# A hybrid decoder layer: the recurrent half's norm goes to all partitions through a scratch row instead of a diagonal product

## The chip, the core and the metric

The kernel runs on one core of a Trainium2 chip. The metric is the device time of one execution in microseconds (us), lower is better. A core has five engines with queues of their own: TensorE (PE; matrix products and transposes, results into the PSUM banks), VectorE (DVE), ScalarE (ACT), GpSimd (POOL) and SyncE (SP), which here issues every transfer. They wait for each other by semaphores. A transfer counts 16 onto its semaphore when it has landed. PEld is TensorE's loading of its stationary operand, which overlaps its products.

## The reference, cut to what matters

One layer over 256 tokens of 2048 channels, float32: a mixer of two halves, then a mixture of experts, each with a residual. The two halves are eight heads of 128 channels of a gated delta rule, and eight blocks of 128 channels of a gated linear recurrence. The change concerns the second half's norm, the last statements here:

```python
h = rms_norm(x, norm_mix_w)
proj = h @ w_in
q, k, v, z, b, a, rx, rgate = split(proj)
y_gdn = gated_deltanet_group(q, k, v, z, b, a, ...)        # 8 heads
# recurrent half, 8 blocks of 128 channels:
log_a = -8 * r * softplus(-lam)
_, h = associative_scan(lru_combine, (exp(log_a), mult * (i * xc)))
y = h * gelu(gate)
y = rms_norm(y per block of 128 channels, norm_w)
x = x + concat(y_gdn, y_rg) @ w_out
x = x + hierarchical_moe(rms_norm(x))                       # 32 experts, top 2
```

## The kernel before, in words

Activations lie transposed: channels on the 128 partitions, the 256 tokens along the row. So the recurrence is a scan along the row, and the norm of a block is a sum over partitions, one number per token, that has to be multiplied into every partition.

The program has a stretch per head h = 0 to 7. In one stretch three things are interleaved on TensorE by an order written out by hand: the delta rule of head h-1 (`heads`), whose triangular system is solved in levels 1 to 6, the projection of head i = h (six blocks b of 128 columns, `project`, 96 steps of three products each), and small work. `fill(n)` puts n projection steps between two products of a level, so that TensorE has work while ScalarE and VectorE treat a level's result. In each level TensorE makes a product P, ScalarE copies it out of PSUM (L1148, `pm`), TensorE makes a product U from it, and VectorE subtracts it (L1584 to level 4, L1589 at level 5, L1592 at level 6). After level 6 TensorE needs VectorE's L1592 for its next product (L678, `bank<-ew,hT` in the views), which also waits for s_mix.

What ScalarE and VectorE do beside a level stands in `between(n)`, n = 0 to 8, run after level n's own instruction. Weight pieces go through a ring of three: SyncE loads 1 MB, ScalarE copies it in two halves into a rounded form (L1039), VectorE writes the rest (L1438), TensorE uses both, and SyncE may load into the slot again when VectorE is done.

The recurrent half of head h-1 passes through this so: VectorE's `recur` (n = 6) leaves y in `yb`, ScalarE squares it (`y_square`), TensorE sums the squares over partitions into one number per token, with the tokens now on the partitions (`square_sums`). In the next stretch ScalarE takes roots (`roots`, n = 2) and VectorE inverts them into `fi` (`invert`, n = 2): columns 0 and 1 for the delta rule, columns 2 and 3 for the recurrent half, 128 tokens each. Then:

- ScalarE, `scaled`, n = 3: `on` is the delta rule's output times its factor (L1096); `dg` is the identity times columns 2 and 3 (L1099), a diagonal matrix per 128 tokens.
- TensorE, `norms`, at level 3: transposes `on` (L643), and multiplies an all-ones matrix with `dg` (L646), which puts the token's factor on every partition, in bank 6.
- VectorE, `finish`, n = 4: two products into `mixT`, one from bank 7 (L1543), one from `yb`, the norm's weight and bank 6 (L1546), then `silu_z` (L1502).

The helpers of TensorE have one line each in the profile: L563 for products, L566 for transposes. Stretch 1 (`body(1, True)`) has no head before it to finish; the stretches 2 to 7 have `body(i, False)`; the last head's levels have their own lists `between`, with w_out pieces in place of w_in, where n = 5 holds `recur` and `add_early(1)` (L1708), for which TensorE waits. The last head's own norm follows behind its levels.

Behind this come the output projection, the router, and the 32 experts, whose weights (12 MB each) are loaded by SyncE in six pieces.

Of the kernel before, what the change touches and what calls it, by code (L numbers as in the profile page):

```python
# [34 lines left out]
NH = 8  # L35
# [93 lines left out]
def build(nc, ins, out, slots=SLOTS):  # L129
# [4 lines left out]
    with ExitStack() as ctx:  # L134
# [62 lines left out]
        pm = R1b.take(NT, P)  # L197
        on = R1b.take(NT, P)
        dg = R1b.take(NT, P)
        sqy = R1b.take(T)  # L200
        yb = R1b.take(T)

# [29 lines left out]
        stat = sb("stat", [P, 8])  # L232
        rows = sb("rows", [16, 3, P])
        gb = R1b.take(3, P)
        rows_d = nc.dram_tensor("decay_rows", (16, 3 * P), F32, kind="Internal").ap()

        xn = mixT[:, :, :].rearrange("p (t k) i -> p t (k i)", t=NT)
# [140 lines left out]
        s_f = sem("s_f")  # L378
        s_on = sem("s_on")
        s_dg = sem("s_dg")  # L380
        s_oT = sem("s_oT")
        s_rb = sem("s_rb")
        s_ph = sem("s_ph")
# [177 lines left out]
        def _(pe):  # L561
# [77 lines left out]
            def norms(h):  # L639

                pe.wait_ge(s_on, h + 1)
                for t in range(NT):
                    l = tr(bank[7][:, T + t * P:T + (t + 1) * P], on[:, t, :])  # L643
                l.then_inc(s_oT, 1)
                pe.wait_ge(s_dg, h + 1)
                mm(bank[6][:, 0:T], ones, dg.rearrange("p t i -> p (t i)"), True, True).then_inc(s_rb, 1)  # L646

            def heads(h, fill, last_done, nxt):

# [361 lines left out]
        def _(act):  # L1011
# [80 lines left out]
            def scaled(h):  # L1092

                act.wait_ge(s_f, h + 1)
                for t in range(NT):
                    l = act.activation(on[:, t, :], bank[7][:, t * P:(t + 1) * P], ACT.Copy, scale=fi[:, t:t + 1])  # L1096
                l.then_inc(s_on, 1)
                for t in range(NT):
                    l = act.activation(dg[:, t, :], ident, ACT.Copy, scale=fi[:, 2 + t:3 + t])  # L1099
                l.then_inc(s_dg, 1)  # L1100

            def values(h):

# [69 lines left out]
            def body(i, first):  # L1173
                h = i - 1

                def between(n):
                    if n == 0:
                        high(h * 6 + 8, 2, h * 2 + 3, (0,))
                    elif n == 1:
                        factors(h)  # L1180
                        high(h * 6 + 8, 2, h * 2 + 3, (1,))
                    elif n == 2:
                        evac(i, 0)
                        if not first:
                            roots(h - 1)
                        key_norms(h)
                    elif n == 3:
                        values(h)
                        if not first:
                            scaled(h - 1)  # L1190
                        high(i * 6 + 3, 0, i * 2 + 2)
                    elif n == 4:
                        evac(i, 1)
                        tanh_half(i, 0)
                    elif n == 5:
                        high(i * 6 + 4, 1, i * 2 + 2)
                    elif n == 6:
                        evac(i, 2)
                        decays(i)
                        tanh_half(i, 1)  # L1200
                    elif n == 7:
                        y_square(h)
                        high(i * 6 + 5, 2, i * 2 + 2)
                    elif n == 8:
                        squares(i)
                        evac(i, 3)
                        high(i * 6 + 6, 0, i * 2 + 3)
                        tanh_half(i, 2)

                heads(h, between)  # L1210
                evac(i, 4)
                high(i * 6 + 7, 1, i * 2 + 3)
                out_squares(h)
                evac(i, 5)
                gelu_square(i)
                gates(i)
# [24 lines left out]
            def between(n):  # L1241
                h = NH - 1
                if n == 0:
                    mix_high()
                elif n == 1:
                    factors(h)
                    high_out(2)
                elif n == 2:
                    roots(h - 1)
                    key_norms(h)  # L1250
                elif n == 3:
                    values(h)
                    scaled(h - 1)
                    high_out(3)
                elif n in (4, 5, 6):
                    high_out(n)
                elif n == 7:
                    y_square(h)
                    high_out(7)
                elif n == 8:  # L1260
                    mix_high_late()
# [124 lines left out]
        def _(dve):  # L1386
# [153 lines left out]
            def finish(h, rgn):  # L1540

                dve.wait_ge(s_oT, h + 1)
                V.scalar_tensor_tensor(mixT[:, h, :], bank[7][:, T:], gnw[:, 0:1], sz, ALU.mult, ALU.mult)\  # L1543
                    .then_inc(s_mix, 1)
                dve.wait_ge(s_rb, h + 1)
                V.scalar_tensor_tensor(mixT[:, h + NH, :], yb, rgn, bank[6][:, 0:T], ALU.mult, ALU.mult)\  # L1546
                    .then_inc(s_mix, 1)
                dve.wait_ge(s_mix, h * 2 + 2)

            def system(h):  # L1550
# [84 lines left out]
            def body(i, first):  # L1635
                h = i - 1

                def between(n):
                    if n == 0:
                        gates(h)  # L1640
                    elif n == 1:
                        factors(h)
                        rest(h * 6 + 8, 2)
                    elif n == 2:
                        params(i)
                        if not first:
                            invert(h - 1)
                        query_norms(h)
                        conv(i, 0)
                    elif n == 3:  # L1650
                        rest(i * 6 + 3, 0)
                    elif n == 4:
                        if not first:
                            finish(h - 1, rgp[:, 0:1])
                            silu_z(h)
                        silu(i, 0)
                    elif n == 5:
                        rest(i * 6 + 4, 1)
                        conv(i, 1)
                    elif n == 6:  # L1660
                        recur(h)
                        silu(i, 1)
                    elif n == 7:
                        rest(i * 6 + 5, 2)
                        conv(i, 2)

                heads(h, between)
                rest(i * 6 + 6, 0)
                silu(i, 2)
                conv_rx(i)  # L1670
                link(V.tensor_copy(rgp[:, :], ph[:, Q_RGN:Q_RGN + 1]))
                norm_sums(i, True)
                head_params(i)
                system(i)
                rest(i * 6 + 7, 1)
# [10 lines left out]
            def rest_out(m):  # L1686
                rest(NH * 6 + m, m % RING)
# [23 lines left out]
            def between(n):  # L1711
                h = NH - 1
                if n == 0:
                    gates(h)
                    mix_rest(2, lambda a: a[:, 8:12, :])
                elif n == 1:
                    factors(h)
                    rest_out(2)
                elif n == 2:
                    invert(h - 1)  # L1720
                    query_norms(h)
                    add_early(0)
                elif n == 3:
                    rest_out(3)
                elif n == 4:
                    finish(h - 1, rgp[:, 0:1])
                    silu_z(h)
                    rest_out(4)
                elif n == 5:
                    recur(h)  # L1730
                    add_early(1)
                elif n == 6:
                    rest_out(5)
                elif n == 7:
                    rest_out(6)
                    add_early(2)
# [95 lines left out]
            link(V.tensor_scalar(slot[:, :, 0:NE], slot[:, :, 0:NE], -1.0, None, ALU.add))  # L1832
            iota = cst[:, C_IO:C_IO + CAP].rearrange("p (a s) -> p a s", a=1)

            def pick(q, t, j):
                blocks = pickr[:, t, j // 2].rearrange("p (b s) -> p b s", b=3)
                s = slot[:, t, bass.ds(q * QUAD + j, 1)]
                if j % 2 == 0:
# [3 lines left out]
            def picks(q):  # L1842

                for t in range(NT):
                    for j in range(QUAD):
                        l = pick(q, t, j)
                l.then_inc(s_pick, 1)

            def gates_of(q):
# [3 lines left out]
            if CAP < SLOTS:  # L1853
                link(V.memset(pick, 0.0))
            V.tensor_reduce(cnt[:, 0:1], bank[5][:, 2 * NE:3 * NE], AX.X, ALU.max).then_inc(s_cnt, 1)
            pick(0, 0, 0)
            dve.wait_ge(s_cnt, 1)
            V.tensor_scalar(cnt[:, 1:2], cnt[:, 0:1], float(CAP), 1.0, ALU.is_gt, ALU.add).then_inc(s_cnt, 1)
            pick(0, 0, 1)
            for q in range(2, T // CAP):  # L1860
                dve.wait_ge(s_cnt, q)
                V.scalar_tensor_tensor(cnt[:, 1:2], cnt[:, 0:1], float(q * CAP), cnt[:, 1:2],
                                       ALU.is_gt, ALU.add).then_inc(s_cnt, 1)
                if q < 4:
                    pick(0, 0, q)
            dve.wait_ge(s_cnt, T // CAP)
            V.tensor_copy(nrounds[:, :], cnt[:, 1:2]).then_inc(s_nr, 1)
            for j in range(QUAD):
                l = pick(0, 1, j)
            l.then_inc(s_pick, 1)  # L1870

            dve.wait_ge(s_route, 1)
# [145 lines left out]
```

## Time and profile before

| | |
|---|---|
| Time, 3 runs | median 1473.07 us (1470.9 to 1474.52) |
| Profiled execution | 1471.94 us, its span 1470.1 us |
| Mean granted TensorE clock | 0.985 |
| TensorE busy | 1355.3 us (92%) |
| VectorE busy | 611.1 us (42%) |
| ScalarE busy | 440.0 us (30%) |
| Transfers | 481.63 MB, mean 328 GB/s |

The span runs from the first to the last instruction. The shares are averages over very different stages: up to about 450 us the heads run, then the output projection and the router, and from about 527 us the experts. A busy time counts instructions, not how well an engine is used; which engine's work ends last in a stage stands in the chain of waits.

### The profile page before, as it was taken

How to read it: one execution, taken by the hardware profiler on the slowest of the kernel's cores; microseconds unless marked ns; L12 is line 12 of the kernel's file. 1: busy time of each engine (PE TensorE's matmuls, PEld its weight loads, DVE VectorE, ACT ScalarE, POOL GpSimd, SP SyncE). 2: the span in 40 equal slices, each digit the busy share in tenths (PEclk: the TensorE clock that was granted, in tenths of full speed). 3: DMA queues.
4: the chain of work that ended last, by engine and by line, in shares of the span. 5: the costliest groups of instructions: out<-in, count | busy, mean ns of one | idle time of the engine just before them, and what ended most of it. 6: DMA issues, size and time to landing. Idle time of an engine off the chain costs nothing.

```text
span 1470.1 us, 20406 instructions
## 1 busy us (share of the span) xinstructions
PE 1355.3 (92%) x7784; PEld 834.5 (57%) x7784; DVE 611.1 (42%) x1136; ACT 440.0 (30%) x865; POOL 65.3 (4%) x63
## 2 busy tenths in 40 slices
PE   4999999999999998899999899899899889999895
PEld 3899999999988743343353343343353344335332
DVE  5977787778855621232223212222222122222323
ACT  5465655656554511111021011020111111102102
POOL 0012220122100000000000000000000000000000
PEclk9999999999999999999999999999999999999999
DMA  7565555455546769999999999999999999999994
GB/s 201 152 155 152 151 148 152 120 150 151 200 144 192 313 261 428 429 428 428 426 428 428 428 429 428 429 428 429 428 428 428 429 428 424 429 428 428 427 428 191
DMA packets 147064, 481.63 MB, mean 328 GB/s; under 512 B 11385, under 2 KB 112978, under 8 KB 121810
## 3 DMA queue, kind: packets, MB, share of 16 engines
q1 hardware_dynamic: 147026, 481.10, 83.8%
q8 instruction: 26, 0.43, 0.1%
q14 instruction: 12, 0.10, 0.0%
HBM read 478.96 MB, written 2.12 MB: 327 GB/s over the span
## 4 chain that ended last, share of the span: by engine, by line
PE 66%; DMA 24%; DVE 5%; ACT 2%; issue 1%; SPq 1%; DVEq 0%; ACTq 0%
PE bank L563 65%; DMA ew<-in_expert_w_dram 23%; PE bank L566 2%; DVE w_parts L1438 1%; ACT ew L1350 1%; DMA fw<-in_norm_ffn_w_dram 1%; SPq L530 0%; DVE fw L1907 0%; ACT fw_r L1277 0%; DVE ew L1477 0%; DVE fw_r L1758 0%; DVE fw L1398 0%; DVE fw L1958 0%; DVE ew L1915 0%; ACT ew L1352 0%
## 5 line engine op out<-in xcount | busy, mean ns | idle before, releaser
L563 PE MATMUL bank<-ew,hT 128*64 128x512 f32 (+1 forms) x1568 | 466.6, 602 | 39.5 <-DMA ew<-in_expert_w_dram 32.3
L563 PEld LDWEIGHTS bank<-ew,hT 128*64 128x64 f32 (+1 forms) x1568 | 156.8, 141 | 336.3 <-issue 336.0
L563 PE MATMUL bank<-act_parts,w_parts 128*128 128x256 f32 x2304 | 308.0, 288 | 1.7 <-DVE w_parts L1438 1.7
L563 PEld LDWEIGHTS bank<-act_parts,w_parts 128*128 128x128 f32 x2304 | 285.1, 191 | 2.9 <-issue 1.4
L563 PE MATMUL bank<-ew 128*64 128x512 f32 (+2 forms) x1120 | 248.8, 574 | 6.8 <-DVE ew L1917 6.8
L563 PE MATMUL bank<-mixT,hT 128*64 128x512 f32 x512 | 227.0, 596 | 0.0
L1915 DVE SCALAR_TENSOR_TENSOR ew<-ew,bank 128x256 f32<-128x256 f32 x32 | 13.5, 421 | 453.9 <-ACT ew L1352 453.9
L563 PEld LDWEIGHTS bank<-ew 128*64 128x64 f32 (+1 forms) x1120 | 84.8, 141 | 147.4 <-issue 137.2
L1438 DVE TENSOR_TENSOR w_parts<-fw,w_parts 128x2048 fp32r<-128x2048 f32 x64 | 147.7, 2312 | 31.5 <-ACT w_parts L1039 30.5
L1367 ACT ACTIVATE ye_r<-bank 64x512 fp32r<-64x512 f32 x128 | 68.8, 585 | 279.6 <-PE bank L563 278.8
L1350 ACT ACTIVATE ew<-bank,gs 128x512 f32<-128x512 f32 x32 | 22.0, 687 | 422.0 <-PE bank L563 422.0
L1039 ACT ACTIVATE w_parts<-fw 128x1024 fp32r<-128x1024 f32 x128 | 128.6, 1053 | 12.5 <-PE bank L563 9.0
L1935 DVE TENSOR_TENSOR cst_r<-bank,ye_r 64x512 fp32r<-64x512 f32 x64 | 41.3, 684 | 112.5 <-ACT ye_r L1367 112.3
L1935 DVE TENSOR_TENSOR act_parts<-bank,ye_r 64x512 fp32r<-64x512 f32 x64 | 41.3, 684 | 99.2 <-ACT ye_r L1367 99.0
L1907 DVE TENSOR_TENSOR fw<-fw,bank 128x512 f32<-128x512 f32 x128 | 77.8, 678 | 0.8 <-PE bank L563 0.8
L563 PE MATMUL bank<-act_parts,fw_r 128*128 128x256 f32 x384 | 71.9, 300 | 1.7 <-DVE act_parts L1840 1.3
L563 PE MATMUL bank<-w_parts,act_parts 128*128 128x512 f32 x288 | 69.7, 395 | 0.3 <-DVE fw L1708 0.3
L563 PEld LDWEIGHTS bank<-mixT,hT 128*64 128x64 f32 x512 | 69.9, 138 | 0.0
L1971 POOL TENSOR_TENSOR hT<-ew,cst 128x256 f32<-128x256 f32 x48 | 54.1, 1160 | 283.1 <-DVE ew L1557 283.1
L563 PEld LDWEIGHTS bank<-act_parts,fw_r 128*128 128x128 f32 x384 | 59.9, 201 | 6.6 <-DVE hT L1896 3.8
L563 PE MATMUL bank<-ye_r,act_parts 128*128 128x512 f32 x128 | 58.2, 455 | 5.3 <-DVE act_parts L1935 3.3
L563 PE MATMUL bank<-hT 128*128 128x128 f32 x416 | 62.0, 274 | 0.0
(245 smaller groups left out, 1088.5 us busy)
## 6 DMA issues: line engine op xcount, KB each, us to landing
ew<-in_expert_w_dram SPq DMA_DIRECT2D x160, 2048.0 KB, 16.1
mixT<-in_expert_w_dram SPq DMA_DIRECT2D x32, 2048.0 KB, 18.5
fw<-in_w_in_dram SPq DMA_DIRECT2D x48, 1024.0 KB, 6.0
fw<-in_w_out_dram SPq DMA_DIRECT2D x16, 1024.0 KB, 5.1
mixT<-in_x_dram SPq DMA_DIRECT2D x1, 2048.0 KB, 7.9
fw<-in_x_dram SPq DMA_DIRECT2D x1, 2048.0 KB, 9.6
out_dram<-fw SPq DMA_DIRECT2D x4, 512.0 KB, 2.7
hT<-decay_rows SPq DMA_DIRECT2D x8, 192.0 KB, 5.7
```

The source lines that it names most:

```text
L563: return nc.tensor.matmul(o, l, r, start=start, stop=stop, skip_group_check=True)
L566: return nc.tensor.transpose(o, i, ident[0:n, 0:n])
L1039: act.activation(wparts[:, slot, 0, cols], raw[:, slot, cols], ACT.Copy).then_inc(s_high, 1)
L1350: act.activation(hs, bank[2][:, :], ACT.Copy, scale=gs[:, j:j + 1]).then_inc(s_hs, 1)
L1367: act.activation(y_hi[side * 64:side * 64 + 64, side ^ (j % 2), i * 512:(i + 1) * 512], bank[4 + i][side * 64:side * 64 + 64, :], ACT.Copy ...
L1438: V.tensor_tensor(wparts[:, slot, 1, :], raw[:, slot, :], wparts[:, slot, 0, :], ALU.subtract).then_inc(s_restD, 1)
L1907: V.tensor_tensor(x2c, x2c, bank[COMB[i % 4]][:, :], ALU.add).then_inc(s_add[t], 1)
L1915: V.scalar_tensor_tensor(eth, eth, 1.0, b3[:, :, 0:SLOTS], ALU.add, ALU.mult).then_inc(s_u, 1)
L1935: l = V.tensor_tensor(y_lo[half][rows, cols], bank[4 + i][rows, :], y_hi[rows, half, cols], ALU.subtract)
L1971: G.tensor_tensor(atm[:, lv], A[:, 1, 0:3:2, :], m.broadcast_to([P, NT, P]), ALU.mult).then_inc(s_atm, 1)
```

## The change

The norm's factor of the heads 0 to 6 no longer passes through `dg` and TensorE. ScalarE writes the two columns of `fi` to a scratch row in device memory (two transfers of 128 numbers), and at n = 4, one level further on, waits for both and issues a transfer that reads the row into all 128 partitions, at the place of `dg`. VectorE's `finish` and `silu_z` move from n = 4 to n = 5 and multiply with that copy. The last head keeps the diagonal product. A helper `pick` is renamed `seat`, which changes nothing in the program that runs.

```diff
+        rr = dg.rearrange("p t i -> p (t i)")
+        norm_d = nc.dram_tensor("norm_row", (1, T), F32, kind="Internal").ap()
+        s_ro = sem("s_ro")
+        s_rr = sem("s_rr")
...
@@ TensorE, norms(h)
-                pe.wait_ge(s_dg, h + 1)
-                mm(bank[6][:, 0:T], ones, dg.rearrange("p t i -> p (t i)"), True, True).then_inc(s_rb, 1)
+                if isinstance(h, int) and h == NH - 1:
+                    pe.wait_ge(s_dg, 1)
+                    mm(bank[6][:, 0:T], ones, dg.rearrange("p t i -> p (t i)"), True, True).then_inc(s_rb, 1)
@@ ScalarE, scaled(h)
-                for t in range(NT):
-                    l = act.activation(dg[:, t, :], ident, ACT.Copy, scale=fi[:, 2 + t:3 + t])
-                l.then_inc(s_dg, 1)
+                if isinstance(h, int) and h == NH - 1:
+                    for t in range(NT):
+                        l = act.activation(dg[:, t, :], ident, ACT.Copy, scale=fi[:, 2 + t:3 + t])
+                    l.then_inc(s_dg, 1)
+                else:
+                    for t in range(NT):
+                        act.dma_start(norm_d[:, t * P:(t + 1) * P].rearrange("a p -> p a"), fi[:, 2 + t:3 + t])\
+                            .then_inc(s_ro, 16)
+
+            def norm_row(h):
+
+                act.wait_ge(s_ro, h * 32 + 32)
+                act.dma_start(rr, norm_d.broadcast_to([P, T])).then_inc(s_rr, 16)
@@ ScalarE, between(n) of the bodies
                     elif n == 4:
+                        if not first:
+                            norm_row(h - 1)
                         evac(i, 1)
                         tanh_half(i, 0)
@@ ScalarE, between(n) of the last head
                 elif n in (4, 5, 6):
+                    if n == 4:
+                        norm_row(h - 1)
                     high_out(n)
@@ VectorE, finish(h, rgn)
-                dve.wait_ge(s_rb, h + 1)
-                V.scalar_tensor_tensor(mixT[:, h + NH, :], yb, rgn, bank[6][:, 0:T], ALU.mult, ALU.mult)\
-                    .then_inc(s_mix, 1)
+                if isinstance(h, int) and h == NH - 1:
+                    dve.wait_ge(s_rb, 1)
+                    r = bank[6][:, 0:T]
+                else:
+                    dve.wait_ge(s_rr, h * 16 + 16)
+                    r = rr
+                V.scalar_tensor_tensor(mixT[:, h + NH, :], yb, rgn, r, ALU.mult, ALU.mult).then_inc(s_mix, 1)
@@ VectorE, between(n) of the bodies
                     elif n == 4:
-                        if not first:
-                            finish(h - 1, rgp[:, 0:1])
-                            silu_z(h)
                         silu(i, 0)
                     elif n == 5:
                         rest(i * 6 + 4, 1)
                         conv(i, 1)
+                        if not first:
+                            finish(h - 1, rgp[:, 0:1])
+                            silu_z(h)
@@ VectorE, between(n) of the last head
                 elif n == 4:
+                    rest_out(4)
+                elif n == 5:
                     finish(h - 1, rgp[:, 0:1])
                     silu_z(h)
-                    rest_out(4)
-                elif n == 5:
                     recur(h)
                     add_early(1)
```

## Rows read from the trace of the kernel before

**Rows 1.** Chain of waits, heads: start us, us, engine and what, line

```profile
176.84 4.11 PE bank L563 x35
...
181.17 41.41 PE bank L563 x339
...
424.38 0.69 DVE fw L1708
425.06 0.14 issue
425.20 23.79 PE bank L563 x113
```

**Rows 2.** Stretches: busy us per engine (instructions), granted clock, DMA share, GB/s

```profile
176.00:222.00 46.00, 46.00 (x381) 45.31 (x380) 35.85 (x64) 27.77 (x60) 7.62 (x7) 1.00 0.57 144
...
600.00:1427.00 827.00, 763.80 (x3656) 329.81 (x3652) 198.01 (x400) 124.23 (x254) 0.00 (x0) 0.98 1.01 428
```

**Rows 3.** Timeline, TensorE, one head: start us, us, line, instruction, count

```profile
181.00 0.60 PE L563 MATMUL bank<-hT,cst 128*128 128x256 f32 x2
181.44 0.61 PE L563 MATMUL bank<-hT 128*128 128x128 f32 x4
...
183.32 0.61 PE L563 MATMUL bank<-hT 128*128 128x128 f32 x4
...
187.44 1.06 PE L563 MATMUL bank<-hT 128*128 128x128 f32 x8
...
194.25 0.39 PE L563 MATMUL bank<-ew,hT 128*128 128x128 f32 x2
```

**Rows 4.** Timeline, VectorE, the same head; in brackets idle time and releaser

```profile
184.79 0.44 DVE L1543 SCALAR_TENSOR_TENSOR mixT<-bank,gnw,ye 128x256 f32 x1
...
186.00 0.42 DVE L1495 SCALAR_TENSOR_TENSOR ew<-ew 128x256 f32<-128x256 f32 x1
188.53 0.69 DVE L1589 TENSOR_TENSOR hT<-hT,bank 128x512 f32<-128x512 f32 x1 [2.12 <-PE bank L563]
189.14 2.29 DVE L1438 TENSOR_TENSOR w_parts<-fw,w_parts 128x2048 fp32r<-128x2048 f32 x1
...
193.17 0.41 DVE L1592 TENSOR_TENSOR hT<-hT,bank 128x256 f32<-128x256 f32 x1
```

**Rows 5.** Timeline, ScalarE, the same head

```profile
178.60 0.71 ACT L1099 ACTIVATE hT<-cst,fi 128x128 f32<-128x128 f32 x2
179.19 2.02 ACT L1039 ACTIVATE w_parts<-fw 128x1024 fp32r<-128x1024 f32 x2
182.08 0.39 ACT L1148 ACTIVATE hT<-bank 128x256 f32<-128x256 f32 x1 [0.87 <-PE bank L563]
...
184.05 0.42 ACT L1062 ACTIVATE ew<-ew 128x256 f32<-128x256 f32 x1
186.21 0.38 ACT L1148 ACTIVATE hT<-bank 128x256 f32<-128x256 f32 x1 [1.74 <-PE bank L563]
186.49 1.99 ACT L1039 ACTIVATE w_parts<-fw 128x1024 fp32r<-128x1024 f32 x2
```

**Rows 6.** Timeline, SyncE's queue, the same head: the next weight load's issue

```profile
183.70 0.38 SPq L479 DMA_DIRECT2D fw<-in_w_in_dram  x1
```

**Rows 7.** Line 493, issues of the decay rows: ns min/median/max, first and last start

```profile
L493 SPq DMA_DIRECT2D hT<-decay_rows x8: 328/1498/1802, 51.0 to 338.8; - x8
```

**Rows 8.** Page, part 6, the same transfers: KB each, us to landing

```profile
hT<-decay_rows SPq DMA_DIRECT2D x8, 192.0 KB, 5.7
```

**Rows 9.** Line 497, the one write to the scratch tensor decay_rows, 24 KB

```profile
DMA to landing us min/median/max: 2.2/2.2/2.2
```

**Rows 10.** Line 484, loads of a gate's weights, 64 KB, eight of them

```profile
DMA to landing us min/median/max: 3.9/4.3/5.6
```

**Rows 11.** Timeline, VectorE, the last head's loop

```profile
421.79 0.69 DVE L1589 TENSOR_TENSOR hT<-hT,bank 128x512 f32<-128x512 f32 x1 [1.15 <-PE bank L563]
```

**Rows 12.** Timeline, TensorE, the last head's loop

```profile
425.20 1.62 PE L563 MATMUL bank<-w_parts,fw_r 128*128 128x512 f32 x6 [0.94 <-DVE fw L1708]
```

More of the change, by code:

```diff
@@ L1833, in _, with seat @@
             iota = cst[:, C_IO:C_IO + CAP].rearrange("p (a s) -> p a s", a=1)
-            def pick(q, t, j):
+            def seat(q, t, j):
                 blocks = pickr[:, t, j // 2].rearrange("p (b s) -> p b s", b=3)
@@ L1845, in picks @@
                     for j in range(QUAD):
-                        l = pick(q, t, j)
+                        l = seat(q, t, j)
                 l.then_inc(s_pick, 1)
@@ L1855, in _ @@
             V.tensor_reduce(cnt[:, 0:1], bank[5][:, 2 * NE:3 * NE], AX.X, ALU.max).then_inc(s_cnt, 1)
-            pick(0, 0, 0)
+            seat(0, 0, 0)
             dve.wait_ge(s_cnt, 1)
             V.tensor_scalar(cnt[:, 1:2], cnt[:, 0:1], float(CAP), 1.0, ALU.is_gt, ALU.add).then_inc(s_cnt, 1)
-            pick(0, 0, 1)
+            seat(0, 0, 1)
             for q in range(2, T // CAP):
@@ L1864, in _ @@
                 if q < 4:
-                    pick(0, 0, q)
+                    seat(0, 0, q)
             dve.wait_ge(s_cnt, T // CAP)
@@ L1868, in _ @@
             for j in range(QUAD):
-                l = pick(0, 1, j)
+                l = seat(0, 1, j)
             l.then_inc(s_pick, 1)
```

## Prediction

> **What bounds the kernel now.** I read the chain of waits first, for the stretch that the change touches (the eight heads, up to some 450 us). From one head to the next it holds TensorE alone: 4.11 us, two small transposes, 41.41 us, and so on every 45.95 us [rows 1]. The table of stretches agrees: in the 46 us of one head TensorE is busy 46.00 us at a granted clock of 1.00 (2.4 GHz), VectorE 35.85, ScalarE 27.77 [rows 2]. So an instruction taken off TensorE in a head is worth its full spacing, and work on the other engines costs nothing until it makes TensorE wait; what has to be read from their timelines is how much room each has. Behind the heads the experts run for some 830 us with the DMA engines at 1.01 of their time, 428 GB/s [rows 2]. Their loads are released by TensorE's and VectorE's earlier work, so the experts as a block start as much later or earlier as the heads end. A shift in the heads reaches the end of the span whole, and is neither multiplied nor absorbed.
>
> How often the change acts: norms(h-1) runs in the bodies i = 2 to 7 (six times) and in the level loop of the last head (once). The eighth norm, behind the last head, stays as it was.
>
> **Removed from TensorE.** The product of ones with dg is two passes of 128x256. Its first starts at 181.00 and the next level's product at 181.44 [rows 3]: 0.44 us per head, seven times, 3.1 us. This is the most that the change can give.
>
> **ScalarE, level 3.** Two scaled copies of the identity go, from 178.60 to 179.19: 0.59 us [rows 5]. Two transfers of 128 x 4 bytes are issued instead. The trace has no transfer issued by ScalarE. SyncE's issue of 128-partition transfers takes 0.33 us at the least and 1.5 us as a median where a weight load was issued just before it [rows 7]. I take 0.37 each, since here SyncE has issued nothing for over a microsecond and its next load comes at 183.70 [rows 6]; below nothing it can't be, as each is an instruction. That is 0.74 for 0.59, +0.15 us. The next evacuation (182.08) had 0.87 us of idle time before it [rows 5]; it is due 0.44 earlier now, so 0.43 is left, and this edit costs nothing. At 1.5 us each it does cost (rival C).
>
> **ScalarE, level 4.** norm_row waits for both row writes and issues the broadcast. Behind it in ScalarE's queue stand the evacuation of a projection, a table load, a tanh, and the evacuation of level 5, on which TensorE waits. An evacuation is followed after 0.28 us (186.21 to 186.49), so norm_row begins at about 182.08 + 0.28 - 0.44 = 181.92, and the level 5 evacuation is due at 186.21 - 0.44 = 185.77. The three between took from 182.36 to 184.05 + 0.42 = 184.47, 2.11 us, which leaves 1.74 us, the idle time in the row [rows 5], and 0.66 more before the VectorE pass at 189.14 would wait for the weight piece that ScalarE ends at 186.49 + 1.99 = 188.48 [rows 4, 5]. The second row write starts at about 178.97. The only small write to a scratch tensor in the trace landed in 2.2 us [rows 9], the loads of 64 KB in the same part of the head in 4.3 [rows 10], the broadcast load in 5.7 [rows 8]. I take 3 us, between the first two and nearer the write: landing at 182.0, a wait of about nothing, and 0.37 for the issue, inside 1.74. Cost: nothing. The bounds are 2.2 (nothing) and 5.7 (rival B).
>
> In the Trainium skill, "Perfetto Trace Analysis", section "DMA Instruction — HWDGE (DVE, Sync)", says that a DMA's semaphore moves only once the write is confirmed, and that this can take surprisingly long when the target is HBM. That speaks against the change, since the scratch row is in HBM: by this rule rival B gains weight. The one such write here shows 2.2 us, on a quiet queue, so the trace neither bears out the long delay nor excludes it under load.
>
> **The broadcast.** 128 KB to 128 partitions, issued at about 182.3, wanted by VectorE at about 193.1. The load of the decay rows, of the same kind and 192 KB, lands in 5.7 us [rows 8] at the most likely; with that it is there at 188. Five microseconds are over, so nothing.
>
> **TensorE's order.** With the product gone everything behind it, level 5 and 6 included, comes 0.44 us earlier. VectorE waited 2.12 us for TensorE before its level 5 update (188.53) [rows 4], so it follows and also moves 0.44 earlier.
>
> **VectorE, the moved finish.** finish and silu_z take 184.79 to 186.00, 1.21 us [rows 4]. At level 4 they were free: behind them VectorE was idle 2.12 us. Now they stand at level 5, behind the subtraction of a weight piece and a convolution. There VectorE has no idle time: from 188.53 it works through to the level 6 update, which starts at 193.17 and ends at 193.58 [rows 4]. TensorE needs that update for the product at 194.25 [rows 3]. A hand-over from VectorE to TensorE takes 0.14 us (in the chain, between the end of L1708 and TensorE's start) [rows 1]. The room is therefore 194.25 - 0.14 - 193.58 = 0.53 us. 1.21 us go into it, both ends having moved by the same 0.44, so TensorE stalls 0.68 us. Bounds: nothing, if the finish found other cover, and 1.21, if there were no room. Later in the head VectorE is behind by 1.21 - 0.44 = 0.77 us against its old times, but it has several idle spells before anything TensorE waits for, 2.12 us in this row alone, so the lag doesn't pile up from head to head.
>
> Per body: -0.44 + 0.68 = +0.24 us, six times +1.4 us.
>
> **The last head's loop.** There -0.44 again. finish and silu_z now stand directly ahead of recur and the add of the early output columns; VectorE goes from its level 5 update at 421.79 straight through to that add, and TensorE already waits 0.94 us for it [rows 11, 12]; the chain of waits passes through this place [rows 1]. So the whole 1.21 us counts: +0.77 us.
>
> **Sum.** 1.4 + 0.8 = +2.2 us. The profiled execution took 1471.94 us (span 1470.1 and 1.8 around it), which gives 1474.1. It lay 1.1 us under the median of the runs, 1473.07, so that in runs as those the forecast is 1475.3 us. A change of under 0.3% (4.4 us) can't be told here from none, so the forecast is "no measurable change, on the slow side": the product's 0.44 us is paid back by a finish at a worse place.
>
> **Rivals.**
> A, *the saving stays*: the finish at level 5 is hidden in the bodies, for instance since the convolution ends earlier than I think. Then six times -0.44 and +0.77: -1.9 us, 1471.2. At the very most all 3.1 us stay: 1470.0. For it: only a small overhang decides. Against: VectorE has no idle time between L1589 and L1592 [rows 4]. Chance 0.10.
>
> B, *slower, by the wait for the row in ScalarE's queue at level 4*. It decides from a landing of some 4.3 us: then ScalarE is still waiting at 183.26, when SyncE issues its next weight load (183.70 less 0.44 [rows 6]), and the broadcast's issue becomes one that follows a weight load, 1.5 instead of 0.37 us [rows 7]. At a landing of 5.7 us: 178.97 + 5.7 = 184.7, issue until 186.2, tanh until 188.3, so the level 5 evacuation is 2.5 us late and ends, handed over, at 188.8, against TensorE's need at 187.44 - 0.44 = 187.00: 1.8 us of stall, and VectorE's pass is 1.9 late. With the finish's +0.24 that is 2.1 us per body, 12.6 in six, and in the last loop some 3 (a body's 2.1 with the add's 0.8 on top): +16 us, 1489. At a landing of 4.5 it is about a third of that. For it: the transfers share 16 engines with the weights, busy over half of their time in these heads, and two of three neighbouring rows are at or over the point. Against: the row of the only write. Chance 0.20. The same section of the Trainium skill says that a hardware-issued transfer waits for a lock on the one descriptor generator and that this time is within the profiled instruction; this would be the reason for 1.5 against 0.33 us, and agrees with rows 7.
>
> C, *slower, by dear issues on ScalarE at level 3*: two at 1.5 us are 3.0 for 0.59, so 2.4 us late, of which 0.43 is idle time and 0.71 TensorE's own room (the product due at 183.32 - 0.44 = 182.88, the copy ready at 181.64 + 0.39 + 0.14 = 182.17). 1.3 us of stall, with +0.24 some 1.55 per body, 9.3 in six, and in the last loop the 0.77 with as much again: +11, 1484. It decides from 0.9 us each. Chance 0.12.
>
> **Chances and range.** Forecast 0.58, with its own range 1472 to 1478. The range for 8 in 10 takes in the saving in full and most of C and B: 1470 to 1487. Faster by over 0.3% would be below 1468.7, beyond the whole saving: 0.04. Slower by over 0.3%, from 1477.5: B 0.20, C 0.10, and the upper end of the forecast 0.05, so 0.35. The same: 0.61.
>
> **What the profile after would show.** Right: no `hT,cst` product in the seven heads; about 0.7 us of TensorE idle per body ahead of the `ew,hT` product behind level 6, with L1592 as the releaser; a head of 46.2 us instead of 45.95; ScalarE's waits at levels 4 and 5 still on TensorE; in the last loop an idle time of some 2.1 us before 425. Wrong, by A: no idle time on TensorE and a head of 45.5. By B: an idle time of ScalarE ended by the row's transfer, with TensorE waiting on ScalarE at level 5, and heads of 47 to 48 us. By C: long transfer issues in ScalarE's queue and TensorE waiting at level 4. What would overturn it all is a head whose length changes through something that I have at nothing, such as slower weight loads beside the 4 byte writes.

## The result and the profile after

The change makes the kernel slower: 1503.57 us median (1501.54 to 1508.06) against 1473.8 us (1470.9 to 1475.27) on the same chip, ratio 1.0207 with a 95% interval of 1.019 to 1.0223. The forecast was 1475.3 us with a range up to 1487. The profiled execution has a span of 1500.5 us against 1470.1. One execution of the last version below fell in a slow state (1566.74 us, granted clock 0.843) and isn't in its ratio.

The chain of waits of the changed kernel, one head (start us, us, engine and what, line), is to be laid beside [rows 1], where the same stretch holds TensorE alone:

```profile
182.57 0.46 PE bank L567 x4
...
183.22 0.33 ACTq L1109
183.55 0.03 ACT ew L1122
183.58 8.96 DMA norm_row<-fi
192.54 0.02 issue
192.56 0.33 ACTq L1115
...
193.40 1.28 ACT L1067
194.68 0.01 issue
194.69 0.42 ACT ew L1067
195.11 0.28 ACT hT L1163
195.39 0.04 issue
195.44 36.75 PE bank L567 x286
232.18 0.22 PE bank L570 x2
232.40 0.46 PE bank L567 x4
```

A transfer has got into the chain: the second row write, issued at 183.58 and landed at 192.54, and behind it everything that stood in ScalarE's queue, which the prediction had named (the table load and the tanh, then the evacuation of level 5). The head lasts 49.83 us (182.57 to 232.40) instead of 45.95.

The timeline of ScalarE in the same head, beside [rows 5]. The evacuation of level 4 has about the same idle time before it as before the change (1.02 us, there 0.87), and the next evacuation (L1063) comes after 5.23 us of waiting for the row's second write:

```profile
184.33 2.03 ACT L1044 ACTIVATE w_parts<-fw 128x1024 fp32r<-128x1024 f32 x2
187.38 0.39 ACT L1163 ACTIVATE hT<-bank 128x256 f32<-128x256 f32 x1 [1.02 <-PE bank L567]
192.56 0.33 ACTq L1115 DMA_DIRECT2D hT<-norm_row  x1
193.00 0.38 ACT L1063 ACTIVATE ew<-bank 128x256 f32<-128x256 f32 x1 [5.23 <-DMA norm_row<-fi]
```

TensorE's timeline, beside [rows 3]:

```profile
186.74 0.61 PE L567 MATMUL bank<-hT 128*128 128x128 f32 x4
...
195.44 1.25 PE L567 MATMUL bank<-hT 128*128 128x128 f32 x8 [2.54 <-ACT hT L1163]
196.35 3.54 PE L567 MATMUL bank<-act_parts,w_parts 128*128 128x256 f32 x15
199.69 0.65 PE L567 MATMUL bank<-hT 128*128 128x128 f32 x4
...
203.86 0.39 PE L567 MATMUL bank<-ew,hT 128*128 128x128 f32 x2
```

and the table of stretches around it (as in [rows 2]; the column behind the engines is the granted clock):

```profile
191.00:193.00 2.00, 1.90 (x17) 1.69 (x15) 0.00 (x0) 0.00 (x1) 0.00 (x0) 1.00 0.50 45
193.00:195.00 2.00, 0.00 (x0) 0.00 (x0) 0.00 (x0) 1.97 (x3) 0.00 (x0) 1.00 0.55 99
...
196.00:198.00 2.00, 2.00 (x14) 2.00 (x13) 1.27 (x2) 1.27 (x2) 0.00 (x0) 0.59 0.91 268
198.00:200.00 2.00, 2.00 (x12) 2.00 (x12) 1.96 (x3) 0.00 (x0) 0.00 (x0) 0.55 0.06 18
200.00:202.00 2.00, 2.00 (x21) 2.00 (x19) 1.93 (x5) 1.62 (x6) 0.00 (x0) 1.00 0.51 95
```

Here is a second price. TensorE did nothing for 2.54 us, and then, though fully busy again, is granted 0.55 to 0.59 of its clock (the lower level, 1.2 GHz, for most of 4 us). The fifteen projection products take 3.54 us; in other heads of this run, at full clock, the same group takes 2.04.

The head adds up from the starts of products before and after. Level 4's P (186.74) to level 5's U (195.44): 6.00 to 8.70, +2.70, the wait. From there to level 6's P (199.69): 2.69 to 4.25, +1.56, the clock, but for 0.1 us (in the two heads without a slow stretch it is 2.79). To the product behind level 6 (203.86): 4.12 to 4.17, +0.05: the finish at its new place costs nothing in this head, as the slow stretch gives VectorE the time. The removed product: -0.44. Sum +3.87 us. The six bodies cost 5.3, 3.9, 3.6, 4.8, 4.0 and 3.5 us, 25.1 in all (from the starts of the chain's pieces of level 3 before and after); the last loop, up to the product that waits for L1731, 4.4. With 0.5 us ahead of the first of them that is 29.9 of the span's 30.4. The experts stage is unchanged: 428 GB/s at 1.01 of the DMA engines' time in both.

Two things can be read from the six bodies side by side. The second write landed after 10.19, 8.96, 9.41, 9.76, 9.11 and 9.32 us, and TensorE then sat idle ahead of level 5's U for 3.79, 2.54, 2.98, 3.33, 2.68 and 2.84: each time the landing less 6.4 to 6.5 us, so that a landing costs from some 6.4 us on. And the bodies without a slow stretch, the third and the sixth, aren't cheap: they cost 3.6 and 3.5 us, since there TensorE waits 0.55 us for VectorE behind the finish (L1615). Beyond the idle time ahead of level 5 a body costs 1.3 to 1.5 us with the slow stretch and 0.6 without.

The landings of ScalarE's transfers (KB each, median us to landing):

```profile
hT<-norm_row ACTq DMA_DIRECT2D x7, 128.0 KB, 6.2
norm_row<-fi ACTq DMA_DIRECT2D x14, 0.5 KB, 7.8
```

For one pair (issued at 183.2 and 183.6) the row "min/median/max" reads

```profile
DMA to landing us min/median/max: 5.0/7.0/9.0
```

so the first write of a pair lands after 5.0 us and the second after 9.0.

### The profile page after: what moved, and what is told of

It reads as the page before. It is cut to its first block, busy times and chain, and to the rows that moved or that the text cites. A ratio compares the mean times of both kernels' runs of the same rounds, so it can differ in the third digit from the quotient of the medians.

```text
span 1500.5 us, 20395 instructions
## 1 busy us (share of the span) xinstructions
PE 1366.9 (91%) x7770; PEld 843.2 (56%) x7770; DVE 612.2 (41%) x1136; ACT 435.8 (29%) x851; POOL 65.3 (4%) x63
## 4 chain that ended last, share of the span: by engine, by line
PE 61%; DMA 26%; DVE 6%; ACT 3%; issue 2%; SPq 1%; ACTq 0%; DVEq 0%
PE bank L567 60%; DMA ew<-in_expert_w_dram 21%; DMA norm_row<-fi 4%; PE bank L570 2%; DVE w_parts L1457 1%; ACT ew L1369 1%; ACT L1067 1%; DMA fw<-in_norm_ffn_w_dram 0%; DVE ew L1496 0%; SPq L534 0%; ACT fw_r L1296 0%; DVE fw L1930 0%; ACT w_parts L1044 0%; DVE ew L1938 0%; DVE fw_r L1781 0%
## 5 line engine op out<-in xcount | busy, mean ns | idle before, releaser
L567 PE MATMUL bank<-act_parts,w_parts 128*128 128x256 f32 x2304 | 312.8, 291 | 1.7 <-DVE w_parts L1457 1.7
L567 PEld LDWEIGHTS bank<-act_parts,w_parts 128*128 128x128 f32 x2304 | 289.9, 194 | 2.8 <-issue 1.4
L567 PE MATMUL bank<-hT 128*128 128x128 f32 x416 | 65.5, 285 | 20.8 <-ACT hT L1163 20.8
L567 PEld LDWEIGHTS bank<-hT 128*128 128x128 f32 x416 | 57.6, 199 | 23.1 <-ACT hT L1163 22.4
```

The lines of the kernel that those rows point to most:

```text
L567: return nc.tensor.matmul(o, l, r, start=start, stop=stop, skip_group_check=True)
```

## The experiments

Each ratio is against the kernel before, run beside it on the same chip, and a difference in us is that ratio times the kernel before's median there (1473.58 to 1474.97 us); the plain medians differ from it by up to 1.1 us. The theory after the result: (1) the wait for the row in ScalarE's queue makes the loss, and the clock that it costs is part of it; without it the forecast's own sum holds. Rivals: (2) the moved finish is the loss; (3) the extra transfers, by their issue or traffic.

**The finish moved, nothing else.**

```diff
@@ VectorE, bodies (the kernel before, s_dg and bank 6 kept)
                     elif n == 4:
-                        if not first:
-                            finish(h - 1, rgp[:, 0:1])
-                            silu_z(h)
                         silu(i, 0)
                     elif n == 5:
                         rest(i * 6 + 4, 1)
                         conv(i, 1)
+                        if not first:
+                            finish(h - 1, rgp[:, 0:1])
+                            silu_z(h)
```

The last head's list is changed as in the change too.

> The kernel before with finish and silu_z one level later in VectorE's order; the diagonal product stays. Theory 1 (the change's cost is the wait for the row in ScalarE's queue): only the forecast's finish term shows, 0.68 us in each of six bodies and 1.21 in the last loop, +5.3 us, some 1479, with TensorE idle 0.5 to 0.7 us behind VectorE's level 6 update. Theory 2 (the finish at its new place is the cost): +25 us or more, near 1500.

Measured: 1480.52 us, ratio 1.0045 (1.0032 to 1.0059), +6.6 us (by the plain medians +5.6). The waits of TensorE in the heads (us in total, times, longest us):

```profile
PE bank L563 <- DVE hT L1592: 2.8, 6, 0.5
PE bank L563 <- DVE fw L1708: 2.5, 2, 2.2
```

A head lasts 46.67 us, +0.72 on 45.95, where +0.68 was worked out; the last loop's wait is 2.2 us where it was 0.94. Theory 2 falls: the finish explains 6 of 30 us, and none on top of the wait where the clock is slow.

**The wait taken away.**

```diff
@@ the changed kernel
+                    act.wait_ge(s_ro, h * 32)
                     for t in range(NT):
                         act.dma_start(norm_d[:, t * P:(t + 1) * P]...
...
-                act.wait_ge(s_ro, h * 32 + 32)
-                act.dma_start(rr, norm_d.broadcast_to([P, T])).then_inc(s_rr, 16)
+                act.dma_start(rr, const[0:1, 0:T].broadcast_to([P, T])).then_inc(s_rr, 16)
```

The broadcast copies constants, so the norm's own factor is left out in the heads 0 to 6.

> The changed kernel, but the broadcast reads 256 numbers of the constants instead of the row just written, so nothing waits for the two row writes, which are still issued (computes the recurrent half's norm of heads 0 to 6 with wrong factors). Theory 1: the wait is gone and what is left is the forecast, +2.2 us, some 1476 (1474 to 1479), ScalarE never idle on a transfer, the granted clock at 1.00 throughout the heads. Theory 3 (the transfers' issues or their traffic beside the weight loads slow the heads by themselves): at or over 1490.

Measured: 1476.43 us, ratio 1.0016 (1.0006 to 1.0025), +2.4 us; the forecast's sum was +2.2. The row writes are all issued and land as late as before, the broadcasts too run (5.6 us), and TensorE waits for VectorE alone, 0.5 us at the most behind level 6, at a granted clock of 1.00 in all heads. A head lasts 46.24 us. The landing of the row writes:

```profile
DMA to landing us min/median/max: 4.6/7.2/10.1
```

So some 28 of the 30 us hang on that one wait, and theory 3 falls.

**One write of 128 x 8 bytes.**

```diff
-                    for t in range(NT):
-                        act.dma_start(norm_d[:, t * P:(t + 1) * P].rearrange("a p -> p a"), fi[:, 2 + t:3 + t])\
-                            .then_inc(s_ro, 16)
+                    act.dma_start(norm_d.rearrange("a (p t) -> (a p) t", t=NT), fi[:, 2:4]).then_inc(s_ro, 16)
...
+                    two = [a.rearrange("q (t p) -> q t p", t=NT) for a in (mixT[:, h + NH, :], yb)]
+                    V.scalar_tensor_tensor(two[0], two[1], rgn, rr.rearrange("q (p t) -> q t p", t=NT), ...
```

> The changed kernel with one write of 128 x 8 bytes in place of two of 128 x 4, the row kept with the two halves of tokens interleaved and read so by VectorE. Theory 1a (the second write lands at 9 to 10 us because it queues behind the first, some 4.5 us per 128 small descriptors): the one write lands at 5.0 to 6.4 us as the first of each pair did; ScalarE waits 0.5 to 2 us, which is about its room; 1475 to 1479. Theory 1b (the landing under load is 9 us whatever is written): ScalarE waits as in the changed kernel and the time stays near 1503.

Measured: 1477.52 us, ratio 1.0021 (1.0011 to 1.0031), +3.1 us. The write lands in 4.2 to 6.2 us (median 5.0), ScalarE waits for it 6.5 us in five times together, 2.1 the longest, and TensorE never waits for ScalarE; a head lasts 46.25 us. The room in ScalarE's queue was at least as large as read.

**What makes the landing long.** Five transfers in the quiet stretch before the first expert:

```diff
@@ ScalarE, the kernel before, behind its wait for s_nr
+            act.dma_start(quiet_d[0, 0:1].rearrange("a p -> p a"), fi[:, 2:3]).then_inc(s_q, 16)
+            act.wait_ge(s_q, 16)
+            act.dma_start(quiet_d[1, 0:1].rearrange("a p -> p a"), fi[:, 2:3]).then_inc(s_q, 16)
+            act.dma_start(quiet_d[1, 1:2].rearrange("a p -> p a"), fi[:, 3:4]).then_inc(s_q, 16)
+            act.wait_ge(s_q, 48)
...
```

> The kernel before with five transfers to a scratch tensor, each waited for by ScalarE, put where the DMA engines are nearly idle (between the router and the first expert): one column of 128 x 4 bytes, two such at once, one of 128 x 8 bytes, 128 rows of 512 bytes, and one row of 1 KB from a single partition. Theory load (the landing is long through the weights' traffic): all land in 2 to 3 us. Theory descriptors (small writes to device memory are slow in themselves): one column about 4.5 to 5, two about 9, 128 x 8 about 5, the 512 byte rows and the single row 2 to 3.

Measured, from one issue to the next, each having waited for the one before: 128 x 4 bytes 7.3 us (the queue's first transfer), two of them 8.2, 128 x 8 bytes 3.4, 128 x 512 bytes 1.7. The weights' traffic isn't needed for a long landing. Neither theory had the sizes right: one column took more than the 4.5 to 5 us expected, and two hardly more than one. (Its one time, 1493.21 us, holds these waits.) With a warm-up, and with the pieces apart:

```diff
+            act.dma_start(quiet_d[1, 0:1].rearrange('a p -> p a'), fi[:, 2:3], ...)
+            act.wait_ge(s_q, 32)
+            act.dma_start(quiet_d[2:3, :, 0].rearrange('a p -> p a'), fi[:, 2:3], ...)
+            act.wait_ge(s_q, 48)
...
+            act.dma_start(quiet_d[5, 0:2].rearrange('b p -> (b p)').rearrange('(p s) -> p s', s=2), fi[:, 2:4])
+            act.wait_ge(s_q, 96)
...
```

> The kernel before with ten transfers by ScalarE to a scratch tensor in the quiet stretch before the first expert, each waited for: a warm-up row; 128 x 4 bytes side by side; 128 x 4 bytes with 512 bytes between; with 64 bytes between; side by side again; 128 x 8, 128 x 16 and 128 x 512 bytes side by side; a row of 1 KB from one partition, twice. Theory count (each of 128 small writes costs its time): the three layouts of 4 bytes land alike. Theory neighbours (many small writes into the same few hundred bytes wait for each other): 4 bytes with 512 between land in about 2 us, side by side in 5 to 7, and 128 x 8 and 128 x 16 lie between by their spread. Theory first use (7.3 us before was the queue's first transfer): the warm-up is slow and the column behind it near 4.

The timeline of ScalarE's queue in that stretch, in the order of the text above (start us, us, line), from a transfer's issue to the next being its landing and the hand-over (0.02 us above, from 192.54 to 192.56):

```profile
515.05 0.49 ACTq L1326 DMA_DIRECT2D quiet<-cst  x1
517.42 0.36 ACTq L1328 DMA_DIRECT2D quiet<-fi  x1
524.52 0.33 ACTq L1330 DMA_DIRECT2D quiet<-fi  x1
525.97 0.33 ACTq L1332 DMA_DIRECT2D quiet<-fi  x1
527.41 0.33 ACTq L1334 DMA_DIRECT2D quiet<-fi  x1
534.11 0.33 ACTq L1336 DMA_DIRECT2D quiet<-fi  x1
537.63 0.33 ACTq L1338 DMA_DIRECT2D quiet<-fi  x1
539.30 0.33 ACTq L1340 DMA_DIRECT2D quiet<-cst  x1
540.88 0.24 ACTq L1342 DMA_DIRECT2D quiet<-cst  x1
541.99 0.23 ACTq L1344 DMA_DIRECT2D quiet<-cst  x1
```

The same 128 pieces of 4 bytes stand here three ways: side by side 7.10 us, starts 512 bytes apart 1.45, starts 64 bytes apart 1.44, and side by side again 6.70. With 8 bytes each, side by side, it is 3.52, with 16 bytes 1.67, and a row of 1 KB from one partition takes 1.11. Neither the number of pieces nor their size alone makes it long, but how close together the small pieces lie. Over what distance they hinder each other isn't shown: nothing between side by side and 64 bytes apart was tried with 4-byte pieces, and 64 bytes, the word of the expectations below, is one guess that fits. The theory of first use falls: the warm-up took 2.37 us, while other transfers still ran, and the column behind it 7.10. The theory of neighbours stands. Each layout was timed once (side by side twice), in one execution of 1500.55 us.

**The same beside the weights.** Two changes to the changed kernel with the wait in its place:

```diff
@@ 64 bytes apart; the broadcast reads constants
-                        act.dma_start(norm_d[:, t * P:(t + 1) * P].rearrange("a p -> p a"), fi[:, 2 + t:3 + t])\
+                        act.dma_start(norm_d.rearrange("a (t p s) -> a t p s", t=NT, s=16)[:, t, :, 0]..., fi[:, 2 + t:3 + t]
@@ 16 bytes each, side by side
+                    act.dma_start(norm_d.rearrange("a (p q) -> (a p) q", q=4), fi[:, 0:4]).then_inc(s_ro, 16)
```

> The changed kernel, its two writes of 128 x 4 bytes, its wait at n = 4 and its broadcast all in their places, but the 4-byte pieces stand 64 bytes apart in the scratch tensor, and the broadcast reads 256 constants (computes the recurrent half's norm of heads 0 to 6 with wrong factors). Theory neighbours (pieces of a few bytes side by side in the same 64 bytes are written one after the other, 1.4 us spaced against 6.7 to 7.1 us side by side in the quiet stretch): both writes land in about 2 to 3.5 us beside the weights too, ScalarE hardly waits, the time is that of the run without the wait, +2.4 us, some 1476. Theory load (beside the weights the count or the traffic makes it slow whatever the spacing): landing 5 and 9 us, near 1503.

> The changed kernel with one write of all four columns of fi, 128 x 16 bytes side by side, a broadcast of 2 KB per partition in place of 1 KB, and VectorE reading every fourth number; all in the change's own places. Theory neighbours: 16 bytes side by side took 1.7 us in the quiet stretch, so the write lands in 2 to 3.5 us, ScalarE doesn't wait at level 4, the larger broadcast lands in time (it has some 10 us), and the time is the forecast's, +2.4 us, some 1476. Theory load: landing 5 us as the 8-byte pieces had, ScalarE idle about 1 us per head, still 1476 to 1478; the landing in the trace tells them apart.

Spaced: 1477.2 us, ratio 1.0021 (1.001 to 1.0033), +3.1 us. The two writes' landing:

```profile
DMA to landing us min/median/max: 1.8/3.6/4.9
```

and ScalarE's wait (us in total, times, longest us):

```profile
ACT ew L1063 <- DMA norm_row<-fi: 2.3, 2, 1.2
```

against 34.3 us in six waits in the changed kernel (and 6.2 in the last loop). Nothing but the distance of the pieces and what the broadcast reads differs from the changed kernel, and the run without the wait had the same constants read beside pieces side by side, landing in a median of 7.2 us. So the long landing in the heads too comes from the pieces lying side by side. Wide: 1478.75 us, ratio 1.003 (1.0016 to 1.0043), +4.4 us, landing 3.1 to 5.1 us, median 3.8, ScalarE waiting 1.5 us in all. Both medians are a little over the 2 to 3.5 us expected, and some 2 us over the 1.44 and 1.67 of the quiet stretch: the place beside the weights has a share in the landing too, though not the one that made the loss. The wide version is somewhat dearer than forecast, since VectorE's product with every fourth number takes 0.68 us instead of 0.48, and all of that is in TensorE's wait (4.1 us in six times, in the spaced run 2.8). The spaced run leaves out the norm's own factor in the heads 0 to 6, the wide one does not.

**The wait one level later, the writes as in the change.**

```diff
@@ ScalarE, bodies, the changed kernel
                     elif n == 4:
-                        if not first:
-                            norm_row(h - 1)
                         evac(i, 1)
...
                         high(i * 6 + 4, 1, i * 2 + 2)
+                        if not first:
+                            norm_row(h - 1)
```

The last loop is that of the kernel before, so this compares with the 25.1 us of the six bodies.

> The changed kernel, two writes of 128 x 4 bytes as there, but the wait and the broadcast stand at n = 5 of ScalarE's list, behind the weight piece; the last loop as in the kernel before. Theory 1 (the price is set by the wait's place in ScalarE's queue, not by the landing itself): the second write has landed before ScalarE comes to the wait, TensorE no longer waits on ScalarE at level 5, the clock stays at 1.00; left are the finish's +0.3 us per body and up to 1.2 us per body in which VectorE waits for the broadcast: +2 to +9 us, 1477 to 1484. Rival (the long landing costs wherever it is waited for): over 1495.

Measured: 1481.43 us, ratio 1.0051 (1.0035 to 1.0066), +7.5 us. ScalarE's arithmetic no longer waits for a transfer, but VectorE does, 3.8 us in three of the heads, and TensorE for VectorE:

```profile
PE bank L567 <- DVE hT L1613: 6.9, 6, 2.9
```

The broadcast is issued 8.9 to 9.9 us after the second write and lands after 4.8 to 7.6 more (median 6.1); in three heads of six that is too late for the finish. One point of the expectation failed: the clock did not stay at 1.00. In the first of these heads TensorE, idle for 2.89 us behind level 6, was granted 0.56 and 0.59 from 152 to 156 us, and this head alone lasts 50.21 us, 4.3 of the 7.5. (In this head one write's issue took 1.50 us too; otherwise none of ScalarE's issues in any run here took over 0.54.) The same landing at another place costs less than a third of what it cost in the bodies.

**A row of 1 KB from one partition beside the weights, nobody waiting.**

```diff
@@ ScalarE, scaled(h), the kernel before
                 l.then_inc(s_dg, 1)
+                if not (isinstance(h, int) and h == NH - 1):
+                    act.wait_ge(s_q, h * 32)
+                    act.dma_start(busy_d[0:1], rows[0:1, 0:2].rearrange("a q p -> a (q p)")).then_inc(s_q, 16)
+                    act.dma_start(busy_d[1:2], rows[1:2, 0:2].rearrange("a q p -> a (q p)")).then_inc(s_q, 16)
```

> The kernel before with two extra writes per head at the place of the row writes, nobody waiting for them, each one row of 1 KB from a single partition. If the long landing comes from the small pieces, these land in 2 to 3 us, although the weights are being loaded beside them; if it comes from the load, in 5 to 9. The time stays within 3 us of before either way.

One time, 1473.69 us beside 1473.58 (1470.91 to 1475.48): this traffic costs nothing that one execution can show. The trace lists no landing for these rows, so the other half of the question was not answered by it; the quiet stretch has 1.1 to 1.3 us for such a row.

**A version made from the first of these results.** It has 8-byte pieces, and the last loop is that of the kernel before.

```diff
@@ ScalarE: one write of 8-byte pieces; the wait behind the weight piece
                     elif n == 5:
                         high(i * 6 + 4, 1, i * 2 + 2)
+                        if not first:
+                            norm_row(h - 1)
@@ VectorE: finish in two
                     elif n == 4:
+                        if not first:
+                            finish_delta(h - 1)
+                            dve.wait_ge(s_mix, h * 2 - 1)
+                            silu_z(h)
                         silu(i, 0)
...
                     elif n == 6:
-                        recur(h)
+                        recur(h, None if first else lambda: finish_rec(h - 1, rgp[:, 0:1]))   # ahead of yb
@@ TensorE
-                    pe.wait_ge(s_mix, h * 2)
+                    pe.wait_ge(s_mix, h * 2 - 1)
```

> Made from what the first runs showed: one write of 128 x 8 bytes, the wait for it and the broadcast one level later in ScalarE's queue (n = 5, behind the weight piece), VectorE's product from bank 7 and silu_z back at n = 4, and only the product with the row at n = 6, behind the level 6 update and three of recur's operations; the last loop as in the kernel before. Theory 1 with its sizes: nothing that TensorE waits for is late, the removed product is saved in six bodies, a head of 45.5 us, -2.6 us against before, some 1472. If a new wait appears (VectorE at the row, or ScalarE behind y_square), the time is at or over before, 1475 to 1479.

Measured: 1470.28 us, the median of eleven, ratio 0.9981 (0.9972 to 0.999): 2.8 us faster than the kernel before, 1.5 to 4.1 by the interval. Its chain in the heads is TensorE's alone again, with a head of 45.52 us:

```profile
180.71 40.97 PE bank L567 x337
221.68 0.22 PE bank L570 x2
221.90 4.11 PE bank L567 x35
226.01 0.22 PE bank L570 x2
```

Beside [rows 1], 41.41 has become 40.97: the 0.44 us of the removed product, six times 2.6 us.

## Why the prediction was wrong

Point by point, by its own steps:

- *TensorE alone bounds the heads, and a shift there reaches the end whole*: right. 29.9 of 30.4 us lie in the heads.
- *Removed product, 0.44 us*: right (40.97 for 41.41).
- *ScalarE, level 3, +0.15 us, nothing*: right in effect, wrong in how. The issues take 0.33 to 0.54 us, but stand at 183.22 and 183.58, ahead of the scaled copies and beside other work: ScalarE's queue issues them while its arithmetic runs. The second one was put at 178.97; counted back by the 5.74 us that this head's level 3 product is later, it came at 177.84, 1.1 us earlier. Rival C falls.
- *ScalarE, level 4, the row lands in 3 us and the wait costs nothing*: this is the step that failed. The second write lands 9.0 to 10.2 us after its issue, three times the 3 us taken, and the wait cost TensorE 2.5 to 3.8 us per body. Both the value and its upper bound of 5.7 were taken from transfers of large pieces (1.5 KB and 512 bytes), and none of these says anything of 4-byte pieces side by side; the size of a piece and its neighbours are part of what has to be alike in a neighbouring row. The range inherited the false bound, and ended at 1487, under even the 1489 of rival B.
- *The room there, 1.74 us and a little*: right. A wait of up to 2.1 us cost TensorE nothing in the run with 8-byte pieces.
- *Rival B*: its place and its queue are what happened. Its point of decision, a landing of 4.3 us, is not: the 8-byte pieces landed in 4.2 to 6.2 us and TensorE never waited for ScalarE, and in the changed kernel the idle time is the landing less 6.4. The 4.3 rested on the broadcast's issue growing to 1.5 us behind a weight load, and it took 0.33 us in all seven, three or more microseconds behind SyncE's issue. Its price was for a landing of 5.7, +16 us. It also left out the clock: after idle times of 2.54 to 3.79 us TensorE was granted the lower clock for some microseconds in four of the six bodies, 1.5 to 1.6 us each time, and in the last loop.
- *The moved finish, 0.68 us per body, 1.21 in the last loop*: right: 0.72 measured alone, and 1.3 more of waiting in the last loop. In the changed kernel it shows only in the bodies without a slow stretch.
- *The sum without the failed step*: +2.2 forecast, +2.4 (0.9 to 3.7) measured in the run without the wait.

## What to carry to other kernels

A wait put into the queue of an engine that also serves the busiest one is worth as much as the latest thing it can wait for, less the room to the next thing that is needed; work out that room, and then ask from which duration it is used up, rather than how long the wait will probably be. A duration for a transfer may be taken from another only if the pieces are alike, in size and in where they land; for a transfer that isn't in the trace the upper bound is open. If a small column must go to device memory, two layouts were fast here: 16 bytes a piece, or starts 64 bytes apart. And put the wait where the data are needed, not a level before. An idle time that is bought on TensorE can be charged twice, the second time in clock.

## What the runs showed of the hardware

- 128 pieces of 4 bytes, one per partition, written side by side to device memory: 6.7 to 7.1 us with the DMA engines idle, 52 to 55 ns per piece; with starts 64 bytes apart 1.44 us. Side by side, 8 bytes each 3.5, 16 bytes 1.7, 512 bytes 1.6 to 1.7, one row of 1 KB 1.1 to 1.3. The Trainium skill, "DMA: Bandwidth & Descriptors", section "Specifications", says that pieces under 512 bytes are read, changed and written back. That rule sorts by size only; here 4 bytes spaced and 16 bytes side by side cost about what 512 bytes do, so size alone doesn't decide. That close pieces wait for each other's turn is what the numbers suggest; within what distance, and where in the path, isn't shown. The profile counts the DMA engines as hardly busy meanwhile: for 0.01 of the time from 527.4 to 534 us, the second such write in the quiet stretch.
- Beside the weights the first of two such writes landed in 5.0 to 6.7 us and the second in 9.0 to 10.2; in quiet two together took 8.2, and one alone 6.7 to 7.3. Why the first of two is often quicker beside the weights than one alone in quiet is open.
- TensorE's clock: in the heads an idle time of 2.54 to 3.79 us was followed in four bodies of six by a stretch at 0.50 to 0.60, as was one of 2.59 in the last loop and one of 2.89 in the run with the wait one level later; in two bodies (2.98 and 2.84 us idle) by none. The length of the idle time doesn't sort them. In the runs without the wait and with 8-byte pieces, where TensorE is idle for 0.5 us at the most in the six bodies, the clock is 1.00 throughout them.
